# One reciprocal of the attention loop, issued after the convolution taps instead of before them

## The reference, cut to what matters

```python
s = jnp.einsum("bqngd,bqknd->bngqk", qg, ksel).astype(jnp.float32) * scale
s = jnp.where(valid[:, None, None], s, -jnp.inf)
p = jax.nn.softmax(s, axis=-1).astype(vsel.dtype)      # attention
o = jnp.einsum("bngqk,bqknd->bqngd", p, vsel)
...
u = causal_depthwise_conv(u, dw_w, dw_b)               # 31 taps, u: (B, T, 1024)
...
merged = (g_attn * jnp.einsum("bte,ed->btd", attn, w_o_attn[l])
          + g_rnn * jnp.einsum("bte,ed->btd", rnn, w_o_rnn[l])
          + g_conv * jnp.einsum("bte,ed->btd", cnv, w_o_conv[l]))
```

## Time and profile before

| | |
|---|---|
| median of 3 runs | 3891.23 us (3887.97 to 3893.17) |
| the profiled execution | 3887.97 us, its span 3886.2 us |
| TensorE matmul busy | 3582.6 us (92%) |
| VectorE busy | 2431.6 us (63%) |
| ScalarE busy | 1005.3 us (26%) |
| GpSimd busy | 2057.5 us (53%) |
| mean granted TensorE clock | 0.956 of full speed |

### The profile page before, as it was taken

How to read it: one execution, slowest core, us unless ns; L and a number is a source line. 1 busy time by engine, 2 the same in 40 slices (tenths; PEclk the granted TensorE clock), 3 DMA queues, 4 the chain that set the end, 5 groups by cost and what they waited for, 6 DMA issues and landing times.

```text
span 3886.2 us, 49881 instructions
## 1 busy us (share of the span) xinstructions
PE 3582.6 (92%) x20100; PEld 3067.2 (79%) x20100; DVE 2431.6 (63%) x2980; ACT 1005.3 (26%) x1772; POOL 2057.5 (53%) x1100
## 2 busy tenths in 40 slices
PE   7999789999999999788899999999987778899997
PEld 7898678899999879666678778778866664588886
DVE  6686899877732757689978853483224544563335
ACT  4306432221110431633131110111023333322201
POOL 4354235565766535423556776676643532366664
PEclk9899899999999989989999999999988888999999
DMA  3122112222322312211223433332333322222232
GB/s 132 49 93 71 33 44 67 66 91 95 130 92 100 102 55 88 65 38 44 76 71 108 141 116 99 118 139 92 103 132 119 116 88 78 74 92 92 97 109 71
DMA packets 96899, 348.31 MB, mean 90 GB/s; under 512 B 10848, under 2 KB 13152, under 8 KB 93664
## 3 DMA queue, kind: packets, MB, share of 16 engines
q1 hardware_dynamic: 80064, 289.44, 22.5%
q10 hardware_dynamic: 16672, 56.70, 3.8%
HBM read 322.32 MB, written 23.79 MB: 89 GB/s over the span
## 4 chain that ended last, share of the span: by engine, by line
PE 64%; DVE 26%; ACT 8%; issue 2%; DMA 0%; POOL 0%; ACTq 0%; DVEq 0%; POOLq 0%
PE acc L473 18%; PE acc L474 18%; PE acc L476 18%; DVE cu L1874 8%; PE aux L624 1%; DVE ptmp L2037 1%; PE aux L773 1%; DVE rh L1830 1%; DVE w L2177 1%; PE acc L723 1%; DVE zz L2207 1%; ACT us L1437 1%; PE aux L694 1%; DVE rb L1827 1%; ACT yv L1471 1%
## 5 line engine op out<-in xcount | busy, mean ns | idle before, releaser
L446 POOL TENSOR_SCALAR whi<-raw 128x1024 fp32r<-128x1024 f32 x548 | 627.4, 1145 | 1754.8 <-PE acc L476 1733.8
L448 POOL TENSOR_TENSOR wlo<-raw,whi 128x1024 fp32r<-128x1024 f32 x548 | 1430.2, 2610 | 45.7
L473 PE MATMUL acc<-nhi,whi 128*128 128x512 f32 (+1 forms) x2776 | 956.5, 353 | 60.9 <-DVE nlo L1608 23.8
L474 PE MATMUL acc<-nlo,whi 128*128 128x512 f32 (+1 forms) x2776 | 948.7, 350 | 0.0
L476 PE MATMUL acc<-nhi,wlo 128*128 128x512 f32 (+1 forms) x2776 | 870.0, 349 | 0.0
L473 PEld LDWEIGHTS acc<-nhi,whi 128*128 128x128 f32 x2776 | 527.6, 190 | 149.0 <-issue 62.8
L473 PE MATMUL acc<-bhi,whi 128*128 128x264 f32 (+1 forms) x1864 | 557.9, 315 | 47.1 <-DVE merged L1969 20.6
L474 PEld LDWEIGHTS acc<-nlo,whi 128*128 128x128 f32 x2776 | 527.2, 190 | 67.7
L474 PE MATMUL acc<-blo,whi 128*128 128x264 f32 (+1 forms) x1864 | 547.7, 310 | 0.0
L476 PEld LDWEIGHTS acc<-nhi,wlo 128*128 128x128 f32 x2776 | 488.3, 190 | 68.4
L1874 DVE SCALAR_TENSOR_TENSOR cu<-cx,par,cu 128x528 f32<-128x528 f32 (+1 forms) x480 | 476.0, 1053 | 0.2 <-issue 0.2
(11 more groups left out here) (351 smaller groups left out, 4576.6 us busy)
## 6 DMA issues: line engine op xcount, KB each, us to landing
raw<-in_w SPq DMA_DIRECT2D x548, 512.0 KB, 3.3
kept_cp<-pcp ACTq DMA_DIRECT2D x4, 1280.0 KB, 6.5
cp<-kept_cp ACTq DMA_DIRECT2D x4, 1280.0 KB, 7.5
kept_ap<-pap ACTq DMA_DIRECT2D x4, 1024.0 KB, 4.0
kept_cs<-pcs ACTq DMA_DIRECT2D x4, 1024.0 KB, 6.4
ap__140<-kept_ap ACTq DMA_DIRECT2D x4, 1024.0 KB, 4.8
cs__150<-kept_cs ACTq DMA_DIRECT2D x4, 1024.0 KB, 4.9
merge_gates<-gout ACTq DMA_DIRECT2D x16, 256.0 KB, 2.5
```

The lines of the kernel that those rows point to most:

```text
L446: pool.tensor_scalar(hi, w, 1.0, 0.0, ALU.mult, ALU.add).then_inc(sem("w_hi"), 1)
L448: pool.tensor_tensor(lo, w, hi.bitcast(F32), ALU.subtract).then_inc(sem("w_split"), 1)
L473: pe.matmul(acc[s][:, f, 0:TH], hi, xh[:, f * TH:(f + 1) * TH], start=a, stop=False)
L474: pe.matmul(acc[s][:, f, 0:TH], hi, xl[:, f * TH:(f + 1) * TH], start=False, stop=False)
```

## The change

VectorE's share(j), the reciprocal of the row sum, is issued at the start of iteration j instead of in iteration j - 1 right behind score(j + 1). Between the two places lie the second group of taps of iteration j - 1 and, at the last tile of a head, the gate and the merged tile. The work of every other engine and its order stay as they are.

```diff
@@ -1952,14 +1952,12 @@
                 dve.wait_ge(sem("br_lo"), (l * 3 + 1) * KD)
                 score(0)
                 score(1)
-                share(0)
                 for j in range(len(items)):
+                    share(j)
                     for _ in range(TAPS_ITEM[l][0]):
                         next(taps, None)
                     if j + 2 < len(items):
                         score(j + 2)
-                    if j + 1 < len(items):
-                        share(j + 1)
                     for _ in range(TAPS_ITEM[l][1]):
                         next(taps, None)
                     if items[j][1] == QT[l] - 1:
```

## The result

The changed kernel takes 3912.74 us (median of 6 runs, 3911.77 to 3916.83) against 3889.19 (6 runs, 3886.87 to 3893.17): ratio 1.0062, 95% interval 1.0049 to 1.0076. It is slower by 23.6 us, and outside the 0.2% that can't be told from no change. The profiled execution took 3915.31, its span 3913.5, so the two traces differ by 27.3 us, 3.7 more than the medians.

What follows compares the result with a forecast made beforehand. In layer 0's mix TensorE and VectorE are both almost full, so who waits for whom inside a head decides. Layer 0 +15.4 and layer 1 +4.8 give +20.2 on 3891.23, so 3911; range 3898 to 3930.

Steps and rivals of the forecast that it cites:

- Tile 1, layer 0, +0.86: Layer 0's mix: TensorE's transposes of tile 1 at 7.62 us after L1968's start instead of 6.76, +0.86 a head.
- Tiles 2 and 3: Layer 0's mix: the later reciprocals delay the transposes by +0.16 to +0.24 at tile 2, +0.2 at tile 3.
- Tile 4, +0.7, or +0.2 if a tap gets ahead of whi: Layer 0's mix: GpSimd's splits block two taps, delaying tile 4's transposes by +0.7, or +0.2 if a tap precedes whi.
- The clock, left out of the forecast and held as a rival at 0.16: Both layers' mix: new TensorE waits lower its clock, five or six more heads lose 2.8 us, +15, 3927; chance 0.16.
- Layer 1, +4.8: Layer 1's mix: steady heads +2.8, head before the first merged tile -1.1, last head +3.1; +4.8 in all, from +2.4.
- The faster rival, 0.08: Layer 1's mix: unblocking L1968 gains 2.15 us in seven heads and shortens TensorE's waits, 3878; chance 0.08.
- The longer subtraction by the strict rule, up to 7 more: GpSimd's subtraction for wlo behind a blocked tap: 0.5 us longer in each of 14 heads, up to 7 more.
- Outside mix nothing moves: All stretches outside the two layers' mix: a sign of the forecast, claiming they keep their length.

Runs made afterwards that it cites:

- tapsonly: Kernel before, with every reciprocal moved behind the second group of taps but kept ahead of the gate and merged tile: 3916.23 us, +26.7.
- onetap: Kernel before, with each reciprocal behind the first tap of the second group instead of ahead of that group: 3882.81 us, -4.4.
- early: Kernel before, with the reciprocal moved ahead of the first taps and ScalarE's scaling ahead of its exponential: 3884.15 us, -5.4.
- fill_after: Changed kernel, with TensorE's waits at tiles 0 and 1 (layer 0) and 1 (layer 1) filled with constant matmuls: 3901.83 us, +15.5 against the kernel before.
- fill_before: Kernel before, with 8 matmuls on constants in TensorE's wait ahead of tile 1 in layer 0: 3884.78 us, -1.6.
- boundary: Kernel before, with only the reciprocal of each head's tile 0 moved behind the gate and merged tile: 3875.80 us, -13.8.
- sgearly: Kernel before, with L1968 (the gate's scaling) ahead of the second taps at a head's last tile, reciprocals unmoved: 3882.06 us, -5.1.
- layer0: Kernel before, with the change made in layer 0 alone: 3903.02 us, +13.5.
- mixbest: Kernel before, with reciprocal and ScalarE's scaling earlier in layer 0, and layer 1's tile 0 reciprocals behind the merged tile: 3875.07 us, -11.3.

## Why the prediction was right, step by step

The time was forecast as 3911 (+20.2) and is 3912.74 (+23.6). The mechanism is the one forecast: the reciprocal behind the taps is late at L1250, and TensorE's transposes wait for it (the waits above, tapsonly, onetap, early). That the sum came so near is luck. In the traces the growth is 27.3, not 20.2: layer 0 was forecast 4.0 too high, layer 1 5.4 too low, and 5.7 outside mix weren't forecast at all. Of these 7.1 us, 3.7 aren't in the medians, and the forecast set out from a kernel before that was 2.0 us slower (3891.23) than its median beside the changed one (3889.19).

*Tile 1, layer 0, +0.86.* Transposes at 7.50 after the mark (523.12 - 515.62), forecast 7.62, before 6.76: +0.74. That the exponential covers what lies before is shown by onetap.

*Tiles 2 and 3.* At 12.18 and 15.68, forecast 12.39 and 16.2: the waits of 0.2 aren't there, in this head or in the other six. So TensorE waits for L1250 at three tiles of a head (0, 1 and 4), not at four.

*Tile 4, +0.7, or +0.2 if a tap gets ahead of whi.* It got ahead: the two taps behind the reciprocal of tile 3 took 1.42, whi 2.39 (530.35), and the blocked pair is the one at 532.84. Transposes at 21.31 (forecast 22.0), after a wait of 0.39. Head at full clock 25.1 (25.2 with the waits filled) against 23.7: +1.4, the lower end of 1.35 to 2.1. So the terms of tiles 2 to 4 were over-sized, layer 0 by about 4: forecast +15.4, measured 0.7 + 10.7 = +11.4.

*The clock, left out of the forecast and held as a rival at 0.16.* It does fall: 5 of 7 heads of layer 0 are 26.6 to 26.9 (the expectation of fill_after says 6), and filling the waits takes 6.5 us away. But the kernel before lost 5.9 to the same thing in layer 0 (fill_before), in three of its seven heads (25.3, 26.3 and 25.8), of which I had counted only one. The rival's price was for heads that fell in addition; in layer 0 the net is +0.6.

*Layer 1, +4.8.* The steps were met: L1968 in 0.4 (0.43), tile 1 at 8.2 (8.07), reciprocal of tile 3 at 19.6 (19.81), its transposes at 20.6 (20.78), head 24.7 (24.83), all after the mark at 1721.16. The score of the next tile 0 came at 15.8 instead of 17.1: the split wasn't in its way. Instead TensorE needed 6.81 for 5.2 from tile 1 to tile 2, at a granted clock of 0.93 in this head, and the split blocked one of the three taps behind the score (3.58 for the three). So the later steps were met by another way than the one forecast. Two of the six heads took 26.1 and 26.2, where my sum had 24.7 for each, and the last one 26.2 instead of 23.6. Measured -1.6 (before the first merged tile, from the first transposes) + 11.8 = +10.2: under-sized by 5.4. By the experiments the 11.8 are 10.1 gained by unblocking and clock (boundary), 14.1 lost by the late reciprocals (fill_after 169.9 against boundary 155.8, both at 0.99 or more), 7.7 lost by the clock. The windows agree: VectorE is busy for 149.3 us of 177.6, so it stands idle for 28.3, where it was 11.2 before.

*The faster rival, 0.08.* Its mechanism was real and in the changed kernel all along: L1968 is unblocked. With the higher clock that comes with it this is worth 8 to 10 us in layer 1 (sgearly, boundary, onetap). It didn't decide because the three taps in front of each reciprocal cost more. What I hadn't seen is that the boundary part alone wins, and that a shift of one tap (0.7 us, onetap) is enough for it.

*The longer subtraction by the strict rule, up to 7 more.* It isn't there: wlo takes 2.39 to 2.74 us in both stretches of the changed kernel.

*Outside mix nothing moves.* This step failed: from the last merged tile of layer 0 to the first transposes of layer 1 the changed kernel needs 5.2 us more (1056.1 against 1050.9). layer0, boundary and the changed kernel have this, tapsonly only 1.4 and early none. The first place where it shows is in mg_att of layer 0, some 53 us behind the merged tile. Five taps in the kernel before, and in the boundary kernel, at the same distance to 0.01 us:

```profile
660.06 4.27 DVE L1874 SCALAR_TENSOR_TENSOR cu<-cx,par,cu 128x528 f32<-128x528 f32 x5
```

```profile
656.50 3.48 DVE L1874 SCALAR_TENSOR_TENSOR cu<-cx,par,cu 128x528 f32<-128x528 f32 x5
```

In the one a tap is blocked by GpSimd's split. In the other it isn't, and there whi comes 0.94 us later behind the merged tile (55.82 in the kernel before, 56.76 in the boundary kernel):

```profile
662.60 1.18 POOL L446 TENSOR_SCALAR whi<-raw 128x1024 fp32r<-128x1024 f32 x1 [8.90 <-PE acc L476]
```

```profile
659.98 1.06 POOL L446 TENSOR_SCALAR whi<-raw 128x1024 fp32r<-128x1024 f32 x1 [9.84 <-PE acc L476]
```

whi waits for TensorE's L476, and TensorE is slower there. In both kernels it has waited 5.5 us just before and runs at the lower clock; in the kernel before this ends 51.3 us behind the merged tile, in the boundary kernel at 53.4. The same stretch of both, 51.5 to 53.3 behind the merged tile, with 17 matmuls at a granted clock of 1.00 and 10 at 0.50:

```profile
658.28:660.08 1.80, 1.80 (x17) 1.80 (x16) 1.73 (x5) 0.00 (x0) 0.00 (x0) 1.00 0.00 0
```

```profile
654.72:656.52 1.80, 1.80 (x10) 1.80 (x10) 1.73 (x5) 0.00 (x0) 0.00 (x0) 0.50 0.00 0
```

All 14 traces divide by it. Where the lower clock ends at 51.0 to 51.9 (before, early, tapsonly, sgearly, fill_before, mixbest), the first transposes of layer 1 come after 1050.9 to 1052.3 us; where it ends at 52.3 to 53.7 (the other eight), after 1055.0 to 1056.2. So this term too is the clock's, read from the traces and not set apart by a run. Why the clock rises sooner in some kernels, and how the difference grows from 1 us there to 5 at the end of the stretch, is open.

## What to carry to other kernels

Before a small instruction is moved, look for who is queued behind its consumer, and how much of the delay another instruction on the consumer's queue covers: here 0.7 us cost nothing, and 1.4 us in one layer with 2.1 in the other cost 24 us in all. Where two engines block each other, count the blocked instruction by its place relative to the other engine's trigger: shifting either by under 1 us moved 8 to 10 us. Where a stretch that nothing was changed in gets longer, compare the granted clock in both traces first. When parts of a change have opposite signs, run each alone: here one part by itself (boundary) beat the kernel before.

## What the runs showed of the hardware

- Two waits of 1.47 and 1.8 to 2.1 us in a head of layer 0, with TensorE busy between and behind them, were followed by slower matmuls in 5 of 7 heads of the changed kernel (granted clock 0.94 in the head). In the boundary kernel, with 1.47 and at most 1.10 us, one of 7 had them (0.93). A single wait of 2.42 to 2.44 was so in three of six heads of the kernel before. Matmuls on constants in the waits kept the granted clock at 0.99 to 1.00 and made a kernel with 140 more matmuls in layer 0's mix (1207 against 1067) 8 to 11 us faster.
- GpSimd's whi is recorded with its own waiting: 1.05 us alone, 1.3 behind the gate's scaling (L1966, 0.43 us), 1.6 to 1.8 behind part of a tap, 2.4 behind two.
- After the same wait of 5.5 us the lower clock ended 51.0 to 53.7 us behind the last merged tile of layer 0 in the 14 traces. With it GpSimd's next split came up to 1.2 us later, and the stretch that followed was some 3 to 5 us longer.
- A VectorE instruction and a GpSimd one that block each other can trade places without a change in VectorE's busy time (154.6 and 154.5 us in layer 1, before and boundary): the gain of 10 us was in what waited behind them.
